# RWKV-7 recurrence on TensorE: form products inside inverse products, head sums by block-of-ones products, a new hand-written order

## The reference

```python
kk = heads(k * k_k); kk = kk / max(sqrt(sum(kk * kk)), 1e-12)      # head sum over 64
k  = k * (1 + (a - 1) * k_a);  b = kk * a
S  = S * w_t + (S @ -kk_t) b_t + v_t k_t ;  out_t = S @ r_t         # scan over frames
out = (out - mean) * rsqrt(var + LNX_EPS) * lnx_w + lnx_b           # head mean and head variance
out = (out + sum(r * k * r_k) * v) * g
```

## Time and profile before

| quantity | value |
|---|---|
| median of 3 runs | 3573.81 us (3572.91 to 3578.58) |
| profiled execution, its own time | 3560.2 us |
| its span | 3558.5 us |
| granted TensorE clock, mean | 0.992 |
| busy: PE, PEld, DVE, ACT, POOL | 96%, 84%, 47%, 38%, 49% of the span |
| recurrence phase | about 414 to 1144 us |

### The profile page before, as it was taken

The page is one execution under the profiler, slowest core; times in us unless marked ns, Lnnn a source line. Parts: engine busy times, 40 slices in busy tenths (PEclk is TensorE's granted clock), DMA queues, the critical chain, the costliest instruction groups (busy, mean ns, idle before and its releaser), DMA issues. The chain is left out here.

```text
span 3558.5 us, 87352 instructions
## 1 busy us (share of the span) xinstructions
PE 3422.9 (96%) x33525; PEld 2982.7 (84%) x33525; DVE 1655.7 (47%) x3032; ACT 1352.8 (38%) x2912; POOL 1743.1 (49%) x1622
## 2 busy tenths in 40 slices
PE   8999899999998999999999999999989999999999
PEld 8999788888886998888888887777769988888887
DVE  7112455555554275444444533333343744445444
ACT  6212444444443133333333434444453333333335
POOL 5443365565554534554545544344343354545455
PEclk9999999999999999999999999999999999999999
DMA  4422201111113111111111144444442111111111
GB/s 155 152 94 82 73 24 38 38 39 38 38 31 115 63 38 48 44 46 47 43 50 43 52 115 102 107 105 96 95 120 66 41 45 45 45 50 42 47 44 73
DMA packets 432743, 233.86 MB, mean 66 GB/s; under 512 B 190979, under 2 KB 417043, under 8 KB 431558
## 3 DMA queue, kind: packets, MB, share of 16 engines
q1 hardware_dynamic: 428882, 215.40, 21.8%
q10 hardware_dynamic: 3572, 14.33, 1.0%
HBM read 187.69 MB, written 47.21 MB: 66 GB/s over the span
## 5 line engine op out<-in xcount | busy, mean ns | idle before, releaser
L2614 DVE TENSOR_TENSOR H<-ps,H 128x512 f32<-128x512 f32 x608 | 419.6, 690 | 463.1 <-PE ps L2277 462.4
L2165 POOL TENSOR_TENSOR split<-work,split 128x512 fp32r<-128x512 f32 x280 | 379.7, 1361 | 493.9 <-ACT split L2436 486.8
L2277 PE MATMUL ps<-split,split 128*128 128x512 f32 x1824 | 514.0, 390 | 0.0
L2330 PE MATMUL ps<-xs,split 128*128 128x512 f32 x1920 | 512.5, 393 | 0.0
L1326 PE MATMUL ps<-arena 64*64 64x64 f32 (+1 forms) x9984 | 401.5, 225 | 16.9 <-issue 5.8
L2330 PEld LDWEIGHTS ps<-xs,split 128*128 128x128 f32 x1920 | 349.9, 188 | 68.1
L2277 PEld LDWEIGHTS ps<-split,split 128*128 128x128 f32 x1824 | 339.9, 188 | 70.9 <-DVE H L2614 0.7
L1326 PEld LDWEIGHTS ps<-arena 64*64 64x64 f32 x9984 | 347.9, 135 | 60.5 <-issue 30.2
L2330 PE MATMUL ps<-split,split 128*128 128x512 f32 x1440 | 366.1, 390 | 0.5 <-issue 0.5
L3204 PE MATMUL ps<-xs,split 128*128 128x384 f32 x1656 | 359.8, 354 | 2.6 <-POOL split L3118 2.6
L601 PE MATMUL ps<-mixed,wsplit_mix 128*128 128x384 f32 x1872 | 331.6, 339 | 7.6 <-DVE mixed L824 7.6
(11 more groups left out here) (325 smaller groups left out, 5908.4 us busy)
## 6 DMA issues: line engine op xcount, KB each, us to landing
work<-in_ffn_w_gu SPq DMA_DIRECT2D x168, 256.0 KB, 2.9
work<-in_ffn_w_down SPq DMA_DIRECT2D x168, 128.0 KB, 2.3
work<-in_cache_v SPq DMA_DIRECT2D x64, 256.0 KB, 3.9
work<-in_cache_k SPq DMA_DIRECT2D x256, 64.0 KB, 2.2
rkv_scratch<-lora ACTq DMA_DIRECT2D x24, 576.0 KB, 2.8
stage_mix<-in_rwkv_w_rkv SPq DMA_DIRECT2D x24, 512.0 KB, 3.8
work<-in_attn_w_qkv SPq DMA_DIRECT2D x24, 512.0 KB, 4.2
h_scratch<-H SPq DMA_DIRECT2D x2, 4608.0 KB, 12.5
```

Of the source, the lines that this page charges most:

```text
L2165: pool.tensor_tensor(w[1], frm, w[0].bitcast(F32), ALU.subtract).then_inc(u_lo, 1)
L2277: last = pe.matmul(full(DOWN + j % 2), w[part][:, (m % 2) * P:(m % 2 + 1) * P], mem.hid[xpart][:, SEG[h]], start=(a == 0), stop=(a == 2))
L2330: last = pe.matmul(full(to), unit(i)[part][:, k * P:(k + 1) * P], operand[xpart][:, k, :], start=(first and k == 0 and a == 0), stop=(k == ...
L2614: dve.tensor_tensor(at, full(DOWN + j % 2), at, ALU.add).then_inc(added, 1)
```

## The change

1. **Joint items.** `joined` merges neighbours in TensorE's list. A second half of a level next to a `form` becomes `both`: the products alternate, `heads`, `cross`, `heads`, `cross`. A first part of a serial step followed by a first half of a level becomes `beside`. A joint item waits for the conditions of both before its first product. The other engines keep separate items.
2. **Head sums in thirds.** `sums` becomes two products of a 64x64 block of ones with 384 columns of squares. The sums then stand in all 64 rows of a head. Three `ksum` and three `vsum` items a pair replace one each; `expanded` goes. VectorE takes maximum and reciprocal of 128x384 (keys) or the reciprocal of 128x384 (variance), ScalarE the root of 128x384 (the variance's root before its reciprocal), and `kexp` and `affine` read SBUF instead of PSUM.
3. **Order.** `FIRST` has 95 letters, with 54 C items (all 30 of pair 0, 24 of pair 1) and 17 forms. `PATTERN` has 165 letters. In the period of a middle pair TensorE's list has 14 `both` and 6 `beside` items.
4. **Loads and buffers.** `load(1)` is issued before the loop, `load(p+2)` after `gate_weights(p)`. `m.pc` has three buffers. The streamed dummy products of pair 0 lose the 22 of `kexp`.

```diff
-    "CCCCCCCCCCCCCCCCCCCCCCBBBEBBCBBCEBBCBBFFCBEFEFEFEFEBFEBBECEFEFBEFFCF")
+    "CCCCCCCCCCCCCCCCCCCCCCBBCCCBBCCCBCBECCBBECBEBCFFECCFBBFCFCCECCFECECBECCFCCCCFECBBEFECBFCBECFFCC")
...
-    "EDEACFCABAEAFCECFACECFADEACFCAECDAFECACDACFCCCECACFBACECDADAEDAAFAAEDFCEAAFAEBAEFBEACCACEBACDEABEABCEABACBBACE"
-    "EBABEFDFAEAABFABEAFBEAAABFEAFECBAEFAAAAEFEBFAEFAFAF")
+    "EADABAEDAEAFDFECADACFBEDAFDECDDDDBFAECFAEABFACEBAFCEACCAEBAAABECCAEFBDAFAECAFBECAFCAAECAECFAFCEACFECBAFCEADAEC"
+    "FEACFCACEBAAAFBEBCFAEBAAECCBFAEBAFAECAAAEBAAFEACEBAECCF")
...
+def joined(items):
...
+        if before and before[0] == "form" and key[0] == "invert" and key[2][2] == 1:
+            out[-1] = ("both", key[1], (key, before))
+        elif before and key[0] == "form" and before[0] == "invert" and before[2][2] == 1:
+            out[-1] = ("both", before[1], (before, key))
+        elif before and before[0] == "step" and before[2][1] == 0 and before[2][0] and key[0] == "invert" and key[2][2] == 0:
+            out[-1] = ("beside", before[1], (before, key))
...
             for p in range(PAIRS):
-                if p + 1 < PAIRS:
-                    load(p + 1)
...
                     gate_weights(p)
+                if p + 2 < PAIRS:
+                    load(p + 2)
...
             def sums(out, squares):
-                for i in range(T // P):
-                    last = pe.matmul(out[:, SUM_COLS * i:SUM_COLS * (i + 1)], squares[:, i * P:(i + 1) * P],
-                                     mem.headones[:, 64 - SUM_COLS // 2:64 + SUM_COLS // 2], start=True, stop=True)
...
+                for lo, hi in halves:
+                    last = pe.matmul(out[lo:hi], mem.headones[lo:hi, lo:hi], squares[lo:hi], start=True, stop=True)
...
+                elif what == "both":
+                    (_, _, (g, l, _)), (_, fp, n) = arg
+                    G = GROUPS[g][1]
+                    pe.wait_ge(q_ready[LINE[g]], levels_before(pr, g) + l)
+                    form_start(fp, n)
+                    for q in range(G):
+                        last = first_update(g, q)
+                        form_part(fp, n, 4 // G * q)
+                        if l < LEVELS[g]:
+                            last = second_update(g, q)
...
                 elif what == "ksum":
...
-                    dve.tensor_scalar(roots(0), head_sums(pb), 1e-24, None, ALU.max).then_inc(piece_free[b], 1)
+                    dve.tensor_scalar(third(m.kkn, arg), pb[:, 0:CW], 1e-24, None, ALU.max).then_inc(piece_free[b], 1)
                     dve.wait_ge(piece_free[b], n + 1)
-                    dve.reciprocal(m.rs[:, 0, :], m.rs[:, 0, :]).then_inc(kinv, 1)
+                    dve.reciprocal(third(m.kkn, arg), third(m.kkn, arg)).then_inc(kinv, 1)
...
                 elif what == "affine":
                     p2 = third(m.post2, arg)
-                    dve.scalar_tensor_tensor(p2, pb[:, 0:CW], vp("lnw", pr), p2, ALU.mult, ALU.mult).then_inc(piece_free[b], 1)
+                    vb, vn = PIECE_OF["vsum", pr, arg]
+                    dve.wait_ge(piece_free[vb], vn + 1)
+                    dve.reciprocal(third(m.post1, arg), third(m.post1, arg)).then_inc(vinv, 1)
+                    dve.wait_ge(vinv, 3 * pr + arg + 1)
+                    dve.scalar_tensor_tensor(p2, p2, vp("lnw", pr), third(m.post1, arg), ALU.mult, ALU.mult).then_inc(scaled, 1)
```

More of the change, by code:

```diff
@@ L842 @@
 NCONST = T + 2 * 320 + 6 * 64 + 2 * 64 + 256 + 4
-SUM_COLS = 56
-PIECES = {"w", "a", "ksum", "kexp", "rk", "center", "vsum", "affine", "gate", "fin", "s0t", "ns", "nst"}
+PIECES = {"w", "a", "ksum", "rk", "center", "vsum", "gate", "fin", "s0t", "ns", "nst"}
 LEVELS = [5, 5, 5, 5, 3]
@@ L998, in prepare_items @@
         out += [("w", o, c), ("a", o, c), ("scan", o, c)]
[L999 to L1003, removed]
+    out += [("ksum", o, c) for c in range(3)] + [("decays", o, c) for c in range(3)]
+    out += [("kexp", o, c) for c in range(3)] + [("k2", o, None), ("b", o, None)] + [("write", o, g) for g in range(NG)]
+    return out + [("rkr", o, None)] + [("rk", o, c) for c in range(3)]
 def finish_items(o):
-    return [("center", o, c) for c in range(3)] + [("vsum", o, None)] + [("affine", o, c) for c in range(3)] + [("gate", o, c) for c in range(3)]
+    return [("center", o, c) for c in range(3)] + [("vsum", o, c) for c in range(3)] + [("affine", o, c) for c in range(3)] + [("gate", o, c) for c in range(3)]
 def last_finish_items():
     o = PAIRS - 1
-    center, vsum, rest = (lambda x: (x[:3], x[3], x[4:]))(finish_items(o))
-    return center + [("ns", o, 1), vsum] + rest[:3] + [("nst", o, 0), ("nst", o, 1)] + rest[3:]
+    center, vsum, rest = (lambda x: (x[:3], x[3:6], x[6:]))(finish_items(o))
+    return center + [("ns", o, 1)] + vsum + rest[:3] + [("nst", o, 0), ("nst", o, 1)] + rest[3:]
+def joined(items):
+    out = []
+    for key in items:
+        before = out[-1] if out else None
+        if before and before[0] == "form" and key[0] == "invert" and key[2][2] == 1:
[4 more added lines that the diff above has]
+            out[-1] = ("beside", before[1], (before, key))
+        else:
+            out.append(key)
+    return out
 def recurrence_order():
@@ L1046, in recurrence_order @@
     for_tensor = list(out)
-    for c, after in enumerate((("vsum", o, None), ("affine", o, 2), ("nst", o, 0))):
+    for c, after in enumerate((("vsum", o, 2), ("affine", o, 2), ("nst", o, 0))):
         for_tensor.remove(("gate", o, c))
@@ L1408, in _ @@
                     pe.wait_ge(kq_ready, pr + 1)
-                    sums(pb, m.k2).then_inc(piece_done[b], 1)
-                elif what == "kexp":
-                    pe.wait_ge(kroot, pr + 1)
-                    expanded(pb, m.kkn, arg).then_inc(piece_done[b], 1)
+                    sums(pb[:, 0:CW], third(m.k2, arg)).then_inc(piece_done[b], 1)
                 elif what == "rk":
@@ L1423, in _ @@
                 elif what == "vsum":
-                    for c in range(3) if pr == PAIRS - 1 else (2,):
-                        cb, cn = PIECE_OF["center", pr, c]
-                        pe.wait_ge(piece_free[cb], cn + 1)
-                    sums(pb, m.post1).then_inc(piece_done[b], 1)
-                elif what == "affine":
-                    pe.wait_ge(vroot, pr + 1)
-                    expanded(pb, m.post1, arg).then_inc(piece_done[b], 1)
+                    cb, cn = PIECE_OF["center", pr, arg]
+                    pe.wait_ge(piece_free[cb], cn + 1)
+                    sums(pb[:, 0:CW], third(m.post1, arg)).then_inc(piece_done[b], 1)
                 elif what == "gate":
@@ L1693, in _ @@
                 e = pr % 2
-                if what in ("ksum", "kexp", "rk", "vsum", "affine", "gate", "ns"):
+                if what in ("ksum", "rk", "gate", "ns"):
                     b, n = PIECE_OF[key]
```

188 lines of the change are left out of this document (106 added, 82 removed).

## The result

The changed kernel takes 3621.76 us (median of 4 runs, 3619.43 to 3626.36) beside 3573.36 us for the kernel before on the same chip (4 runs). The ratio is 1.0135, with a 95% interval of 1.0117 to 1.0152: 48 us slower, outside my range of 3500 to 3600. The profiled execution has a span of 3624.6 us, 66.1 more than before, and a mean granted clock of 0.979. Only 48 us of these 66 are the change's: the trace of the kernel before is of a fast execution (3560.2 us, where the median is 3573.4), and that of the changed kernel is of its slowest (3626.36). Keep this in mind wherever a time from the trace before is compared.

What follows compares the result with a forecast made beforehand. TensorE sets the pace; start +17.5, pair 0 -10.6, pairs 1 to 5 -16.5, pair 6 -14.4, pair 7 and end +9 make together -15 us, so a median of 3559 us, 8 in 10 within 3500 to 3600.

Steps and rivals of the forecast that it cites:

- The blocks on VectorE: Middle pair: TensorE waits behind queued wide reciprocals of 2.5 us each, in two blocks, 10 us a pair.
- affine block: Middle pair: three affine items and gate take 10.5 us on VectorE against 5.3 of TensorE work; wait 5 us.
- key block: Middle pair: three ksum items of 3.05 us take 11.9 us against 6.7 of TensorE work; wait 5.2 us.
- The head sums on TensorE: Middle pair: sums and transposes of 7 us become six thirds, 3.9 us; 3 us less, plus 2.5 us off waits.
- Net gain: 9 us: Middle pair: joint items save 12.6 and about 2 us of TensorE occupation, less 5.2 us of overlap already there.
- rival D: Four tiles don't last: a joint item takes 1.4 us; +20 us, 3594; chance 0.09.
- 9 stay: Middle pair: TensorE's other waits, 11.5 us before, less 2.5 us around transposes and full-array sums, leave 9 us.
- the forecast of 82: Middle pair: 63 us TensorE occupation, 9 of waits and 10 for the blocks make 82 us, 3.3 less than now.
- Start: Up to the first serial result: +5.5 us to the first write, +12 for 24 items of pair 1; +17.5 us.
- Pair 0: First pair: no affine block and 8 us less occupation than a middle pair; 70 us for 80.6, -10.6.
- pair 6: Pair 6: key work already done, no key block, 5 us less work; 72 us for 86.4, -14.4.
- C: Rival, VectorE's reciprocals decide: 3.3 us each in the two blocks and the start; +23 us, 3597; chance 0.28.

Runs made afterwards that it cites:

- e4: Changed kernel with both wide reciprocals replaced by a multiply-add giving a constant, so key norm and variance are not applied; 3546.91 us, ratio 0.9935.
- e11: Changed kernel with only the key norm's three reciprocals replaced by a constant-giving operation, those of the variance kept; 3585.48 us, ratio 1.0035.
- e8: Kernel before plus a burst of 1024 alternating, then 512 diagonal products ahead of the recurrence; run for its trace alone, 764 alternating products took 27.9 ns each.
- e10: Changed kernel with no wide reciprocals and no joint items; 3547.39 us, ratio 0.9929.
- e16: Changed kernel without reciprocals, whose joint items wait for both conditions but take one kind of product after the other; 3556.25 us, ratio 0.9953.
- e3: Changed kernel with the joint items taken apart, in the same new order; 3631.05 us, ratio 1.0171.
- e15: Kernel before, in its old order, with head sums in thirds and roots by grouped logarithms and exponentials on ScalarE; 3623.56 us, ratio 1.0144.
- e1: Changed kernel with the old head sums, keeping the new order, joint items, loads and buffers; 3606.73 us, ratio 1.0098.
- e6: Changed kernel with the three affine items of a pair set apart by two or three other items each; 3659.96 us, ratio 1.0251.
- e9: Changed kernel with each reciprocal square root made on ScalarE as a logarithm and an exponential, no reciprocal on VectorE; 3620.18 us, ratio 1.013.
- e13: Changed kernel with roots by logarithm and exponential on ScalarE, a block's three logarithms before its three exponentials; 3569.4 us, ratio 0.9992.

## Why the prediction was wrong

The step that failed is the net gain of 9 us a pair from joint items. The runs show none without the reciprocals and 1.7 us with them. The price of the reciprocals, which decides whether the kernel loses at all, came nearly as forecast.

**The blocks on VectorE: right.** A reciprocal took 2.55 us for my 2.5; VectorE is busy 61.7 us in a middle pair for my 64. The affine block's wait is 4.5 for 5, the key block's 4.6 for 5.2. Taking both away gave 8.8 us a pair for the 10 forecast (e4), in shares of 3.7 and 5.1 (e11). `kexp` took 0.87 for 0.8, `affine` 0.62. From pair 7's first serial result to the last gate it was +4 us where I had +9.

**The head sums on TensorE: 3 us right, the 2.5 us of waits beside them not found.** TensorE is busy 5.0 us a pair with them, where the earlier trace rows has 7.7. Without reciprocals and joint items the pairs 1 to 5 take 81.8 us in the mean, 3.5 less than in the trace before and 4.7 less than in e8 (e10). The head sums were to give 3, and I had taken 2.5 more off the waits. The new order is in these 3.5 too, so this step isn't shown by itself.

**"Net gain: 9 us" for joint items: this step failed, by nearly all of it.** Its condition, that four tiles keep going for a whole item, holds for one item. That is why rival D (a joint item takes 1.4 us) looked wrong in the timeline. But I took TensorE's occupation for the only limit, and priced each item by itself. Over a pair its instructions come at 256 in 3.4 us at best (e8), and a middle pair, 2166 products with as many weight loads, needs 17 such packets, so by my estimate at least 58 us (17 x 3.4) of its 80 to 90 even if the packets came without a pause. Where work stands close together, alternation only runs TensorE into the end of what has been delivered. Without reciprocals the joint items took 6.1 us of busy time off a pair and nothing off its length (e10 against e4), and alternation was worth 9 us in all (e16). With the reciprocals in they gave 1.7 us a pair and 9 us in all (e3). That the supply caps four tiles is shown (e8). That it takes the whole 9 us a pair is not: the gaps behind packets grew by 36 of the 63 us that were forecast for pairs 0 to 6, "issue" by 26.5 of the 37.5 us that the idle time grew by, and the rest are waits for VectorE's adds and POOL's left factors.

**"9 stay" for other waits: failed with it.** They were 11.5 before by my count, and I let them shrink while TensorE's work shrank. In e4, where no block stands, gaps of over 0.2 us between the starts of TensorE's weight loads add up to 28 to 36 us in each of pairs 1 to 5, in e10 to 23 to 24, and before to 23 to 24 as well: the order alone freed none, and joint items added what they saved. A middle pair in steps, forecast and by the traces: joint items with their edges -7.5, measured +0.9; sums and the waits beside them -5.5, measured -3.5; reciprocals +10, measured +8.8. (These three add up to the measured 91.5 because they are differences of the same traces. Taken the other way round, by e3, reciprocals cost 11.4 and joint items give 1.7.) So of the 9.5 us that the forecast of 82 is short, 8.4 are the joint items'.

**Start: mis-sized, +17.5 against 27.5.** In place of +5.5 up to the first `write` stand 12.2 up to the first form. 5.4 of them are projections at half clock ahead of the sums, which the prediction hadn't, and which didn't occur in all runs of this order. From the first sum on it is 6.8 for my 5.5. The path was another than mine: `k2` on POOL waits for the third sum, which VectorE takes behind two reciprocals (439.3 for 427.75). The stretch with the 24 items of pair 1 grew by 15.3 for my 12.

**Pair 0 (-10.6) and pair 6 (-14.4): failed for the same reason as the middle pairs.** Their differences to a middle pair were -12 and -10 by my steps and are -8.0 and -8.4. The middle pair they started from was 9.5 us too short. In sum, the profiled execution missed by 81 us: 10 in the start, 13.5 in pair 0, 47 in pairs 1 to 5, 11 in pair 6, and -1 behind. The median missed by 63 (3621.8 for 3559).

**Two readings in the working.** The head sums with their transposes are put at 8.6 us busy, and the earlier trace rows has 4.4 + 3.3 = 7.7. With their 7 us of occupation the list adds up to 85.2, not 86, and the waits to 12.8 us, not 11.5. And "two forms start 1.73 us apart, so a form costs 0.87" holds only because the earlier trace rows stand at half clock there: at full clock a form's 24 products start within 0.85 us in a middle pair of the kernel before. Neither changes the outcome.

**The rivals.** The sign was C's and D's, the mechanism neither's. C wanted reciprocals of 3.3 us, D single items of 1.4; D's title, "four tiles don't last", is the nearest, though they fail over some hundred products and not over a few. What was to stay outside the range was cheap or still dearer reciprocals, and no case in which TensorE's saved work turned into waits. Two of the signs of being wrong that I had named did come: middle pairs over 86 us and a start longer by more than 23.

**What stays open.** e15 against the kernel before: the thirds in the old order make pairs of 93 us, and its trace shows TensorE waiting for VectorE's L1849 (6.1 us in a middle pair), but which move of the new order avoids it is open. The new order with the old sums and without joint items was not run, so how much of e1's 33 us is the order and how much the joint items is not told apart. e1's trace has TensorE idle 74 us in pairs 0 to 6, where 27 stand before: 24 are "issue", 21 wait for POOL's left factors. The moved loads and the third `m.pc` buffer were not run alone either; no gap of TensorE ends with a DMA.

## What to carry to other kernels

A gain on the bounding engine is a gain in time only as far as the next limit: before pricing an overlap of small products, count instructions per microsecond and compare with what the trace's instruction packets deliver. A busy time that falls while the window stays, with more "issue" time, is the sign of it here. On an in-order engine a long operation costs where it is queued, so look for the other engines that carry the same list (POOL's affine items in e6) before moving it, and group activations by table.

## What the runs showed of the hardware

- TensorE's instructions arrive in packets of 16 KB, 256 instructions, in no run less than 3.2 us apart. In a burst with nothing to wait for (e8) they came 3.4 us apart but for one, 3.57 in the mean, and this held 64x64 products on four tiles at 27.9 ns each, near the 29.1 of two tiles, though between the pauses they start every 14.7 ns. It explains "issue" gaps that end about 1.4 us after a packet lands.
- A wide reciprocal costs 6.6 ns a column (2.55 us for 384), 4.7 times the 547 ns of `tensor_scalar` over the same columns. The slope from 2 to 18 columns, 6.3 ns, had told it.
- Logarithm and exponential loaded a table each time they followed one another (1.28 us); e9 and e13 differ by 51 us, and in nothing but the order of these activations, which takes ScalarE's table loads between 500 and 1050 us from 72 to 30.
